# Second layer's attention with exponentials and values in two rounded halves, and its modulation summed in the first layer's feed-forward part

## What is computed

```python
def block_attention(q, k, v, scale):
    def one_block(qi):
        s = jnp.einsum('bqhgd,bkhd->bhgqk', qi, k, preferred_element_type=jnp.float32) * scale
        p = jax.nn.softmax(s, axis=-1)
        return jnp.einsum('bhgqk,bkhe->bqhge', p.astype(v.dtype), v)
...
for l in range(DEPTH):
    mod_ctx = (silu_ctx @ w_ada[l] + b_ada[l])[None, None, :]
    mod_lat = (silu_c @ w_ada[l] + b_ada[l])[:, None, :]
...
shift1, scale1, gate1, shift2, scale2, gate2 = jnp.split(mod, 6, axis=-1)
h = rms_norm(x, g1) * (1 + scale1) + shift1
x = x + gate1 * token_mixers(h, ...)
h = rms_norm(x, g2) * (1 + scale2) + shift2
x = x + gate2 * ((jax.nn.silu(h @ w_gate) * (h @ w_up)) @ w_down)
```

## Time and profile before

| what | value |
|---|---|
| median of 3 runs | 3691.17 us (3688.93 to 3691.19) |
| profiled execution | 3689.86 us, its span 3688.0 us |
| PE busy | 3449.7 us, 94% of the span |
| DVE busy | 1737.5 us, 47% |
| ACT busy | 735.7 us, 20% |
| POOL busy | 789.6 us, 21% |

### The profile page before, as it was taken

How to read it: one execution, slowest core, us unless ns; L and a number is a source line. 1 busy time by engine, 2 the same in 40 slices (tenths; PEclk the granted TensorE clock), 3 DMA queues, 4 the chain that set the end, 5 groups by cost and what they waited for, 6 DMA issues and landing times.

```text
span 3688.0 us, 49530 instructions
## 1 busy us (share of the span) xinstructions
PE 3449.7 (94%) x17888; PEld 2968.0 (80%) x17888; DVE 1737.5 (47%) x2758; ACT 735.7 (20%) x1334; POOL 789.6 (21%) x430
## 2 busy tenths in 40 slices
PE   7898899998989999999979988999988999999998
PEld 3887655556989999999969875555587999999998
DVE  1645566665163334333354366666534344333433
ACT  2322233333120000000032132333313000000001
POOL 1211111112222222222122101111121322222220
PEclk8997899998999999999989898999999999999999
DMA  5243633423111111111023335424120111111111
GB/s 186 73 146 105 178 96 114 119 77 88 43 35 45 43 36 45 45 34 45 23 59 118 118 125 149 122 84 125 51 87 29 52 45 34 45 45 34 45 34 51
DMA packets 297200, 279.70 MB, mean 76 GB/s; under 512 B 63922, under 2 KB 243908, under 8 KB 297076
## 3 DMA queue, kind: packets, MB, share of 16 engines
q1 hardware_dynamic: 268468, 242.74, 22.6%
q10 hardware_dynamic: 28608, 35.40, 2.6%
HBM read 230.20 MB, written 48.02 MB: 75 GB/s over the span
## 4 chain that ended last, share of the span: by engine, by line
PE 85%; DVE 8%; issue 2%; DMA 2%; ACT 1%; SPq 1%; POOL 0%; ACTq 0%; DVEq 0%; POOLq 0%
PE ps L1664 22%; PE ps L1666 22%; PE ps L1665 22%; PE ps L1917 9%; PE ps L1940 4%; DVE neg_max L1514 3%; PE ps L1705 2%; DVE h_lo L1299 1%; PE ps L1960 1%; PE ps L1726 1%; PE ps L1902 1%; PE ps L1901 1%; PE ps L1690 1%; PE ps L1949 1%; DVE wk L1289 1%
## 5 line engine op out<-in xcount | busy, mean ns | idle before, releaser
L1664 PE MATMUL ps<-h_hi,w_hi 128*128 128x384 f32 (+1 forms) x3072 | 1061.5, 346 | 79.8 <-DVE h_lo L1299 63.8
L1665 PE MATMUL ps<-h_lo,w_hi 128*128 128x384 f32 (+1 forms) x3072 | 1040.9, 339 | 0.0
L1666 PE MATMUL ps<-h_hi,w_lo 128*128 128x384 f32 (+1 forms) x3072 | 1040.2, 339 | 0.0
L1664 PEld LDWEIGHTS ps<-h_hi,w_hi 128*128 128x128 f32 (+1 forms) x3072 | 580.8, 189 | 95.3 <-issue 74.6
L1665 PEld LDWEIGHTS ps<-h_lo,w_hi 128*128 128x128 f32 (+1 forms) x3072 | 580.7, 189 | 11.3 <-issue 0.7
L1666 PEld LDWEIGHTS ps<-h_hi,w_lo 128*128 128x128 f32 (+1 forms) x3072 | 580.1, 189 | 3.2
L1606 DVE SCALAR_TENSOR_TENSOR x<-ps,lmod,x 128x384 f32<-128x384 f32 (+2 forms) x768 | 365.9, 512 | 317.7 <-PE ps L1666 317.6
L1628 DVE TENSOR_TENSOR wk<-ps,wk 128x384 f32<-128x384 f32 x132 | 73.6, 558 | 829.7 <-PE ps L1666 825.2
L1140 ACT ACTIVATE p_t<-ps 128x512 f32<-128x512 f32 (+1 forms) x456 | 264.7, 580 | 506.3 <-PE ps L1666 267.2
L1206 ACT ACTIVATE wk<-ps 128x384 f32<-128x384 f32 x132 | 64.7, 492 | 1468.5 <-PE ps L1666 1468.5
L1664 PE MATMUL ps<-act_hi,w_hi 128*128 128x384 f32 x1056 | 356.9, 338 | 0.0
(11 more groups left out here) (249 smaller groups left out, 4140.8 us busy)
## 6 DMA issues: line engine op xcount, KB each, us to landing
ada_buf<-in_w_ada SPq DMA_DIRECT2D x96, 512.0 KB, 6.2
w_stage<-in_w_ffn_gate SPq DMA_DIRECT2D x44, 512.0 KB, 3.8
w_stage<-in_w_ffn_up SPq DMA_DIRECT2D x44, 512.0 KB, 3.8
w_stage<-in_w_ffn_down SPq DMA_DIRECT2D x44, 512.0 KB, 3.8
s_in<-ev_p ACTq DMA_DIRECT2D x66, 192.0 KB, 1.9
w_stage<-in_w_in SPq DMA_DIRECT2D x24, 512.0 KB, 3.9
ada_w<-in_w_ada SPq DMA_DIRECT2D x4, 2048.0 KB, 17.2
w_stage<-in_w_out SPq DMA_DIRECT2D x16, 512.0 KB, 4.9
```

Of the source, the lines that this page charges most:

```text
L1664: nc.tensor.matmul(out, wh, xh, start=first, stop=False)
L1665: nc.tensor.matmul(out, wh, xl, start=False, stop=False)
L1666: return nc.tensor.matmul(out, wl, xh, start=False, stop=last)
```

## The change

**Second layer's products.** ACT takes each exponential twice, once rounded to fp32r (`p_hi`) and once in full (`p_full`); DVE subtracts them (`p_low`: `p_lo = p_full - p_hi`). DVE also splits the values of each head (`v_halves`). On PE the fp32 product of a step becomes `v_hi` by `p_hi`, `v_lo` by `p_hi`, and one step later `v_hi` by `p_lo` (`product_low`). The three buffers have three slots each and lie in the weight ring, where `ada_buf` was. The scores of step `i+2` now wait for `p_full` of step `i` (the second exponential). The first layer's heads keep the fp32 product.

**Modulation.** Layer 1's heads have none. Layer 0's heads make 9 chunks (4 to 11 of layer 0, and 11 of layer 1), none in the first pair and none in the last head. Chunks 0 to 10 of layer 1 are made in layer 0's feed-forward part, one per chunk: 16 loads of 128 KB in a ring of four, 32 DVE instructions of 256 columns (`next_ada`) placed behind the first five activation tiles, 8 tiny matmuls before down product 4 (`turn`), and a bias addition before addition 10 (`mod_add`). POOL's splits of `w_out` wait for nine chunks in both layers.

**Loops.** The loop over layers is written out on every engine, and layer 1's loop over pairs too.

```diff
+SPLIT_LAYERS = (1,)
+LATE_HERE = 9
+F_TILES, F_RING, F_W = 16, 4, 256
+F_AFTER = ((0, 4), (4, 7), (7, 10), (10, 13), (13, 16), (16, 16))
...
+        p_full = place("p_full", [P, 3, 512], F32, ring_at + 4096)
+        p_hi = place("p_hi", [P, 3, 512], F32R, ring_at + 4096 + 3 * 2048)
+        p_lo = place("p_lo", [P, 3, 512], F32R, ring_at + (RING + 1) * 4096)
...
+                def load_next_ada(q, first=False):
+                    for n in range(F_TILES):
+                        if n >= F_RING or not first:
+                            sp.wait_ge(f_mac, (q * F_TILES + n - F_RING + 1) * 2)
...
+                    with sp.Fori(2, CHUNKS) as c:
+                        for j in range(3):
+                            load_ffn(c, j)
+                        load_next_ada(c - 1)
+                        for j in range(3, 6):
+                            load_ffn(c, j)
...
-                pool.wait_ge(late_ev, (l + 1) * NHEADS)
+                pool.wait_ge(late_ev, LATE_HERE)
...
+                    if l in SPLIT_LAYERS:
+                        st = split_step(y, i)
+                        slot = st % 3
+                        if st >= 3:
+                            act.wait_ge(lo_done, st - 2)
+                        nc.scalar.activation(p_hi[:, slot, 0:w], s_bank(half, i)[:, 0:w], ACT.Exp).then_inc(exp_done, 1)
+                        nc.scalar.activation(p_full[:, slot, 0:w], s_bank(half, i)[:, 0:w], ACT.Exp).then_inc(exp_full, 1)
+                        return
...
-            with dve.Fori(0, DEPTH) as l:
+            for l in range(DEPTH):
...
+                def p_low(y, half, i):
+
+                    st = (y - (l - SPLIT_LAYERS.index(l)) * NHEADS) * STEPS + i
+                    slot = st % 3
+                    _, w, _ = step_of(i)
+                    dve.wait_ge(exp_full, st + 1)
+                    if st >= 3:
+                        dve.wait_ge(pv_mm, y * STEPS + i - 2)
+                    nc.vector.tensor_tensor(p_lo[:, slot, 0:w], p_full[:, slot, 0:w], p_hi[:, slot, 0:w].bitcast(F32),
+                                            ALU.subtract).then_inc(lo_done, 1)
+
+                def pair_split(p, first=False, last=False):
+                    for half in range(2):
+                        y = l * NHEADS + 2 * p + half
+                        more = not (half and last)
+                        for i in range(STEPS):
+                            t = i - MAX_AT - 1
+                            if more and 0 <= t < MAX_TILES:
+                                max_tile(y + 1, t)
+                            p_low(y, half, i)
+                            if more and i == 0:
+                                highs(y + 1, p + half, half == 1)
+                            if more and i == 2:
+                                v_halves(p + half, 1 - half, first=first and not half)
...
-                ada_add(HEADS - 1, 1, l * NHEADS + NHEADS - 1)
...
+                        for i in range(*F_AFTER[j] if l == 0 else (0,)):
+                            next_ada(c, i)
                     for d in range(G * DK):
+                        if l == 0 and d == 10:
+                            dve.wait_ge(f_mm, c + 1)
+                            mod_add(1, c, 7).then_inc(f_ev, 1)
...
+                            if l in SPLIT_LAYERS:
+                                if i:
+                                    product_low(y, half, i - 1)
+                                elif half or not first:
+                                    product_low(y - 1, 1 - half, STEPS - 1)
                             if i + 2 < STEPS:
                                 scores(y, p, half, i + 2)
...
+                        if l == 0 and d == 4:
+                            pe.wait_ge(f_mac, (c + 1) * F_TILES * 2)
+                            turn(f_acc, 7).then_inc(f_mm, 1)
```

More of the change, by code:

```diff
@@ L426, in build @@
         late_loaded = [sem(f"late_loaded{i}") for i in range(2)]
+        f_loaded = [sem(f"f_loaded{i}") for i in range(F_RING)]
+        f_mac, f_mm, f_ev = sem("f_mac"), sem("f_mm"), sem("f_ev")
+        exp_full, lo_done, v_high, v_done = sem("exp_full"), sem("lo_done"), sem("v_high"), sem("v_done")
         late_mac, late_mm, late_ev = sem("late_mac"), sem("late_mm"), sem("late_ev")
@@ L972, in norm_x @@
                         root_x(g + 1)
-            with act.Fori(0, DEPTH) as l:
+            for l in range(DEPTH):
                 act.wait_ge(lay_ready, l + 1)
@@ L1180, in _ @@
                 pair(0, first=True)
-                with act.Fori(1, 5) as p:
-                    pair(p)
+                if l in SPLIT_LAYERS:
+                    for p in range(1, 5):
+                        pair(p)
+                else:
+                    with act.Fori(1, 5) as p:
+                        pair(p)
                 pair(5, last=True)
@@ L1551, in pair @@
                             highs(y + 1, p + half, half == 1)
-                        if half or not first:
-                            ada_add(p - 1 + half, 1 - half, y - 1)
+                        ada_add(p - 1 + half, 1 - half)
                         ada_sums(p, half, 0, 3)
@@ L1571, in _ @@
                     max_tile(l * NHEADS, t, first=True)
+                if l in SPLIT_LAYERS:
+                    v_halves(0, 0, first=True)
                 pair(0, first=True)
                 pair(1)
-                with dve.Fori(2, 5) as p:
-                    pair(p)
+                if l in SPLIT_LAYERS:
+                    for p in range(2, 5):
+                        pair(p)
+                else:
+                    with dve.Fori(2, 5) as p:
+                        pair(p)
                 pair(5, last=True)
-                ada_add(HEADS - 1, 1, l * NHEADS + NHEADS - 1)
                 dve.wait_ge(sums_loaded, (l + 1) * 16)
@@ L1710, in sum_squares @@
                     sum_square(n0, i, *divmod(i, DK))
-            with pe.Fori(0, DEPTH) as l:
+            for l in range(DEPTH):
                 def unit(u, n):
@@ L1919, in products, with product_low @@
                                      stop=(i + 1 in GROUP_END)).then_inc(pv_mm, 1)
+                def product_low(y, half, i):
+                    j = 2 if i == STEPS - 1 else i // 9
+                    _, w, kt = step_of(i)
+                    pe.wait_ge(lo_done, split_step(y, i) + 1)
+                    nc.tensor.matmul(ps[0:VD + 1, GROUP_BANK[j], 0:w], v_half[half][1][:, kt, 0:VD + 1],
+                                     p_lo[:, split_step(y, i) % 3, 0:w], start=False, stop=(i + 1 in GROUP_END))\
+                        .then_inc(pv_mm, 1)
                 def max_scores(y, half, t, first=False, after_ada=None):
@@ L1951, in max_rows, with turn @@
                     ins.then_inc(row_tr, 1)
-                def ada_turn(w, n):
-                    pe.wait_ge(late_mac, (n + 1) * MACS)
+                def turn(acc, bank):
                     settle(pe)
@@ L1966, in pair @@
                         y = l * NHEADS + 2 * p + half
-                        ada = half or not first
+                        before = (p - 1 + half, 1 - half)
+                        ada = has_late(l, *before)
                         more = not (half and last)
@@ L1987, in _ @@
                 pair(0, first=True)
-                with pe.Fori(1, 5) as p:
-                    pair(p)
+                pair(1)
+                if l in SPLIT_LAYERS:
+                    for p in range(2, 5):
+                        pair(p)
+                else:
+                    with pe.Fori(2, 5) as p:
+                        pair(p)
                 pair(5, last=True)
-                pe.wait_ge(late_ev, (l + 1) * NHEADS - 1)
-                ada_turn(1, l * NHEADS + NHEADS - 1)
+                if l in SPLIT_LAYERS:
+                    product_low(l * NHEADS + NHEADS - 1, 1, STEPS - 1)
                 def rc_rows(q):
```

166 lines of the change are left out of this document (124 added, 42 removed).

## The result

| what | before | after |
|---|---|---|
| median (lowest to highest) | 3691.18 us of 4 runs (3688.93 to 3693.19) | 3725.25 us of 4 runs (3718.77 to 3728.74) |
| span of the profiled execution | 3688.0 us | 3723.8 us |
| layer 1's heads, first exponential to last product | 419.7 us | 451.7 us |
| layer 0's feed-forward part, first to last rounded activation tile (`act_hi`) | 783.0 us | 803.1 us |

The ratio is 1.0089, 95% interval 1.0075 to 1.0103. The change makes the kernel 34 us slower; 3720 was forecast.

A forecast was written before the change was run, and what follows sets the result against it. PE, busy 94% of the span, was taken as the bound. Layer 1's heads (-28-19+8+54+6) gave +21 us, the rest (-3.4+19-6-2) +7.6: together +29 on 3691.2 us, forecast 3720 us, range 3685 to 3750.

The forecast's parts named there:

- the mechanism that decides: Layer 1's heads: POOL's two subtractions hold DVE's `p_low`, PE stands still 4.9 us a head in eleven heads, +54 us.
- Rival A: Layer 1's heads: POOL does not hold DVE's subtractions, or DVE gets turns between; kernel at 3659 to 3665 us; 13%.
- B: Layer 1's heads: one hold per head instead of two, the other falling where PE has slack; 3693 us; 10%.
- The splits of `w_out`: Layer 1's second-last head: POOL's earlier splits make three more holds of up to 2.4 us, +6 us (0 to 10).
- The removed modulation: Heads without their turns of 1.7 us: eleven inside layer 1's heads, -19 us; two in layer 0's, -3.4 us.
- the eleven added turns: Layer 0's feed-forward part: eleven turns of 1.7 us between down products of a busy PE, +19 us (16 to 23).
- rival C: Layer 1's heads: standstills drop PE's clock to the lower level for a while, +30 us, kernel 3750 us; 10%.
- the product's gain: Layer 1's heads: three fp32r matmuls for one fp32 product save PE 0.2 us in 139 steps, -28 us.
- ACT's cost: Layer 1's heads: second exponential plus copies show at a head's start, 0.7 us in eleven heads, +8 us (0 to 15).
- between the layers: Start of layer 1: the written-out loop removes DVE's wait behind the jump back, -2 us (0 to -3).
- behind the heads: Behind each layer's last head: earlier splits of `w_out` save 3 us each layer, -6 us.
- D: Layer 0's feed-forward part: DVE falls behind from late loads, a 2 us wait in each chunk, 3742 us; 4%.

The follow-up runs named there:

- e1_no_lows: The changed kernel with POOL's subtractions for layer 1's queries and keys cut to 8 columns from the second pair on; 3671.34 us (one run).
- e4_late_out: The changed kernel with layer 1's first three splits of `w_out` on POOL held until all subtractions of exponentials are done; 3719.02 us, ratio 1.0079 to the kernel before.
- e2_lows4: The changed kernel with each of POOL's four subtractions per pair in layer 1 cut into quarters, all work done; 3695.81 us, ratio 1.000 to the kernel before.
- e5_tiny_plow: The changed kernel with DVE's subtraction of exponentials cut to 8 columns from the fourth step of layer 1 on; 3689.67 us (one run).
- e8_all: The changed kernel with POOL's subtractions in quarters, values' halves at step 15, layer 1's splits of `w_out` behind the heads; 3667.39 us, ratio 0.9934 to the kernel before.
- e3_fp32: The changed kernel with layer 1's fp32 product and single exponential as before, everything else as changed; 3670.69 us, ratio 0.9944 to the kernel before.
- e9_one_turn: The changed kernel with one tiny matmul in place of the eight of each turn in layer 0's feed-forward part; 3717.91 us (one run).
- e7_v_late: The changed kernel with DVE's two instructions on the values moved from step 2 to step 15; 3726.43 us (one run).

## Why the forecast came out

**Right, with its size,** was the mechanism that decides. Two `p_lo` in each of eleven heads are held, 3.13 and 3.40 us, each ending 0.56 us behind a POOL subtraction. Forecast was 4.9 us a head; `e1_no_lows` gives 6 x 4.04 + 5 x 5.73 = 52.9 us, forecast 54. The one figure fits neither kind of head, only their mean. Rival A is out, and B: PE waits for both holds. The splits of `w_out` cost 6.3 (forecast 6), which `e4_late_out` confirms. The removed modulation gave 20.6 in layer 1 (19) and 3.9 in layer 0 (3.4), and the eleven added turns cost 19.7 (19): the term left out the 0.09 us that the matmul behind a turn takes longer. Layer 1's heads by themselves: -20.6 - 12.4 + 52.9 + 6.3 leaves 5.8 us of the +32.0.

**The clock, rival C, came true in part,** where the forecast had it at zero in the sum and 10% as a case. The clock falls in eight of the eleven heads that have holds, for 48 us in all. Six of them, each with 6.8 us at the lower level, take 0.7 to 1.5 us longer than others of their kind (MLA heads without a fall, and a GQA head with one of 3.4 us, since none has no fall): 6.0 us together. That is the missing rest, and a fifth of the 30 us priced in C. PE waits for the maxima's chain soon after, which absorbs much of the slow stretch. The length of a standstill doesn't decide it alone: in two MLA heads the clock falls 0.5 and 1.0 us behind a standstill of 1.37 us, and in two others with the same standstills it stays up. It falls five times in `e2_lows4` (standstills up to 2.4 us), and not at all in the heads of `e5_tiny_plow` (up to 1.85) and `e8_all` (up to 0.56). What decides stays open.

**The terms that were mis-sized are the product's gain and ACT's cost:** -28 and +8, so -20, where 12.4 were measured. By the starts of the exponentials in `e1_no_lows` and `e3_fp32`, a step that gains does so by 0.16 us, not 0.2: the three fp32r products take 0.69 us (a step of 1.15 less 0.46 for the two products of scores) to 0.77 (the rows above), where 0.66 was taken. And of the 11 steps counted, seven gain in an MLA head and three in a GQA head. ACT costs less than feared: the first three steps of an MLA head take 4.57 us against 4.17 in fp32, those of a GQA head 3.52 against 3.70, some 1.3 us in twelve heads with the product's gain in these steps already in it. The 7.6 us too little there and the clock's 5.8 are what makes the heads +32 and not +21.

**What came out better** than forecast: outside the three large stages the kernel gains 5.3 (where 2 was taken) between the layers, the turn there left aside, 3.2 and 3.6 behind the heads (3 and 3), and 3.0 in the rest of layer 1's output projection, for which nothing was forecast and no experiment was made. With that the errors cancel to 5 us in 3725: the sum was nearer than two of its terms, and that is luck, since nothing ties the errors in the heads to those gains.

**D came true in one chunk:** in the first PE waits 1.3 us for the sums (row above), and no forecast term had it. In the others PE is busy without a gap, while DVE does its 32 sums each. A window of layer 0's feed-forward part:

```profile
1500.00:1850.00 350.00, 350.00 (x2039) 350.00 (x2038) 190.73 (x386) 19.39 (x33) 82.58 (x48) 1.00 0.21 64
```

The rule of the Trainium skill that was weighed ahead of the forecast (SBUF — State Buffer, Who interferes with whom: whoever issues first keeps the other out completely) agrees with the rows of the change: each held `p_lo` ends 0.56 us behind a POOL subtraction. `e2_lows4` adds that the one kept out has the next turn.

## What to carry to other kernels

Before putting a DVE instruction with two SBUF operands on PE's path, look at which POOL instructions run in that time: it costs the rest of the POOL instruction, however small it is itself. Cutting POOL's work into pieces as short as DVE's slack, and keeping DVE's queue short in that stretch, turned a loss of 0.9% into a gain of 0.7%; either alone gave at most a part. Most of that gain is there without the split heads (0.6% in `e3_fp32`), so ask first what the part that causes the trouble is worth at its best: 6 us here. And take the gain of a cheaper matmul only for steps that PE sets, by their measured distance and not by the sum of parts.

## What the runs showed of the hardware that I had not expected

- A held instruction and its holder take turns when both queues are full: in a GQA head POOL's second subtraction stands behind DVE's held one, and lasts 3.36 us instead of 2.90.
- A cast of 640 columns with a single SBUF operand was held too (3.25 us for 0.48), while the reductions from PSUM stayed at 1.36 us, even where they ran beneath POOL's subtractions all the while (`e8_all` at 2455.72).
- PE has two paces for one and the same chain of 384-column matmuls at a granted clock of 1.00: 173 ns each, or alternately 174 and 179. It changes between one set of six tiles and the next and can stay to the loop's end (nine chunks in `e9_one_turn`, 1.0 us each) or go after one chunk (the second of the change). Six gate and up tiles in a chunk show it, 8.32 or 8.48 us apart. In `e2_lows4` and `e7_v_late` it filled layer 1's feed-forward part, 11 us. What sets it stays open.
